# Modulation computed four column tiles at a time, and some loads and steps of row group B rescheduled

## The reference, cut to what matters

```
m = silu(c) @ w_ada + b_ada            # w_ada 2048 x 12288, split into sh1 sc1 gt1 sh2 sc2 gt2
h = rmsnorm(x, g1) * (1 + sc1) + sh1
q, k, v, u, g = split(h @ w_in)        # w_in 2048 x 5120
att = three dilated windows of attention, 8 heads; the samples also read a cache of 2048 positions
mix = concat(att, gelu(u) * spatial_mix(layernorm(gelu(g))))
x = x + gt1 * (mix @ w_out)
h2 = rmsnorm(x, g2) * (1 + sc2) + sh2
idx, gate = top 16 of 16384 experts for each row and each of 8 heads, from h2 @ w_query
x = x + gt2 * sum over the 128 chosen (gate * gelu(h2 . expert_u[idx])) * expert_v[idx]
y = rmsnorm(x, g_final)
```

## Time and profile before

| | us |
|---|---|
| median of 3 runs | 3915.32 (3914.49 to 3929.38) |
| the profiled execution's own time | 3915.24 |
| its span, first to last instruction | 3913.5 |

### The profile page before, as it was taken

One profiled execution on the slowest core, in us unless ns is written; L12 is line 12 of the kernel. 1 busy time (PEld: TensorE's weight loads), 2 busy tenths in 40 slices (PEclk: granted clock), 3 DMA queues, 4 the chain that ended last, 5 costly groups with the idle time before them and its releaser, 6 DMA issues.

```text
span 3913.5 us, 27375 instructions
## 1 busy us (share of the span) xinstructions
PE 2883.8 (74%) x8370; PEld 1221.3 (31%) x8370; DVE 2571.7 (66%) x3880; ACT 613.6 (16%) x1431; POOL 1643.8 (42%) x1178
## 2 busy tenths in 40 slices
PE   6999897979999966677779788855555555555555
PEld 2333443643334333233333255511111111111110
DVE  3200114896677878555555677899988998777676
ACT  1000211210111122233310011211111111000010
POOL 2000001434443455333344364455556665566554
PEclk9999998989999978888889889977877777777778
DMA  9899755899999999999999999999999999999997
GB/s 355 304 328 334 273 193 217 343 408 385 412 412 412 393 390 415 420 419 419 419 407 379 415 397 413 417 420 420 419 418 411 401 413 420 419 420 420 420 416 305
DMA packets 305618, 1506.76 MB, mean 385 GB/s; under 512 B 25343, under 2 KB 25343, under 8 KB 155559
## 3 DMA queue, kind: packets, MB, share of 16 engines
q0 software_dynamic: 160048, 1150.87, 71.8%
q1 hardware_dynamic: 142306, 336.46, 23.1%
q10 hardware_dynamic: 3120, 17.70, 1.1%
HBM read 1490.31 MB, written 13.80 MB: 384 GB/s over the span
## 4 chain that ended last, share of the span: by engine, by line
DMA 46%; PE 40%; issue 6%; DVE 5%; POOL 1%; ACT 1%; SPq 0%; POOLq 0%; DVEq 0%; ACTq 0%
DMA arena<-in_expert_v_dram,arena 39%; PE ps L915 12%; PE ps L734 8%; PE ps L515 7%; PE ps L684 4%; DMA arena<-in_w_in_dram 3%; PE ps L616 3%; POOL arena L2145 1%; DMA arena<-in_w_ada_dram 1%; PE ps L727 1%; PE ps L503 1%; DMA arena<-in_w_out_dram 1%; DMA arena<-in_w_query_dram 1%; PE ps L473 1%; DVE arena L1861 1%
## 5 line engine op out<-in xcount | busy, mean ns | idle before, releaser
L915 PE MATMUL ps<-arena 128*128 128x512 f32 (+1 forms) x2176 | 1373.3, 770 | 829.8 <-DMA arena<-in_expert_v_dram,arena 806.4
L1913 DVE CUSTOM_DVE_ANT_0 arena<-arena 128x2048 f32<-128x2048 f32 x544 | 1246.3, 2291 | 416.9 <-DMA arena<-in_expert_u_dram,arena 411.7
L2145 POOL DMA_INDIRECT arena<-in_expert_v_dram,arena x544 | 901.5, 1657 | 1089.2 <-PE ps L915 843.0
L915 PEld LDWEIGHTS ps<-arena 128*128 128x128 f32 (+1 forms) x2176 | 452.0, 225 | 1667.3 <-issue 1444.4
L2145 POOL DMA_INDIRECT arena<-in_expert_u_dram,arena x544 | 696.2, 1280 | 600.8 <-DVE arena L1913 364.9
L1861 DVE SCALAR_TENSOR_TENSOR arena<-arena 128x1024 f32<-128x1024 f32 x539 | 691.4, 1283 | 240.3 <-issue 216.4
L734 PE MATMUL ps<-arena 128*128 128x512 f32 x896 | 401.9, 602 | 0.0
L1298 ACT ACTIVATE arena<-arena 128x128 f32<-128x128 f32 (+1 forms) x544 | 204.3, 392 | 1096.1 <-PE ps L915 951.8
L515 PE MATMUL ps<-arena 128*128 128x512 f32 x640 | 287.5, 607 | 6.0 <-DMA arena<-in_w_in_dram 6.0
L734 PEld LDWEIGHTS ps<-arena 128*128 128x128 f32 x896 | 166.8, 191 | 238.2 <-issue 237.3
L684 PE MATMUL ps<-arena 128*128 128x288 f32 (+1 forms) x896 | 213.8, 398 | 3.1 <-DMA arena<-in_w_query_dram 1.8
(11 more groups left out here) (228 smaller groups left out, 1525.0 us busy)
## 6 DMA issues: line engine op xcount, KB each, us to landing
arena<-in_w_ada_dram SPq DMA_DIRECT2D x96, 1024.0 KB, 14.2
arena<-in_w_in_dram SPq DMA_DIRECT2D x80, 1024.0 KB, 13.8
arena<-in_w_query_dram SPq DMA_DIRECT2D x36, 1024.0 KB
arena<-in_w_out_dram SPq DMA_DIRECT2D x32, 1024.0 KB, 5.1
arena<-in_cache_k_dram SPq DMA_DIRECT2D x24, 1024.0 KB
arena<-in_cache_v_dram SPq DMA_DIRECT2D x24, 1024.0 KB, 13.2
arena<-in_expert_u_dram,arena POOLq DMA_INDIRECT x544
arena<-in_expert_v_dram,arena POOLq DMA_INDIRECT x544
```

Of the source, the lines that this page charges most:

```text
L915: ins = MM(ps[0:rows, c, :], diag[t % 4][:, 0:rows], v_slot[t % RING][:, c * NC:(c + 1) * NC], start=(j == 0), stop=last, skip_group_check ...
L1913: V.tensor_tensor_reduce(out=u_slot[s % RING], in0=u_slot[s % RING], in1=h2[b], scale=1.0, scalar=0.0, op0=ALU.mult, op1=ALU.add, accum_ou ...
L2145: nc.gpsimd.indirect_dma_start(out=slot[s % RING], out_offset=None, in_=table, in_offset=bass.IndirectOffsetOnAxis(ap=idx, axis=0),).then_ ...
```

## The change

- `w_ada` is read in six **groups** of four tiles. A load is now one block of 128 weight rows by 2048 columns (`ada_source`: pieces of 8 KB; groups 0 and 1 take 1024 columns of the shift part and 1024 of the scale part, pieces of 4 KB). The four column groups of the array take the same block of rows with four different tiles (`ada_block`), and the sum over 16 blocks builds up in the bank. There is no copy to `partial` and no fold: DVE adds the bias for all four tiles at once from the bank (`ada_group`), with bias and gain rows laid out over 128 partitions. Block 0 of group n waits until DVE has done group n-1 (`mod_ready`).
- The turn is four [128, 128] pieces for a group, with four copies, and `quarter_ready` comes in two steps instead of four.
- The list is mixed finely: 16 blocks of group 0, four times (4 blocks, one `w_in` quarter), and then each of the 28 remaining `w_in` quarters behind two or three blocks.
- DVE's index tables are made before the first group and behind the second.
- Group B's first norm moves from step 4 to step 13 (`T_NORM1`), the second head's choice of block 0 from step 1 to step 5 (`TOP_0`), and the loads of B's x rows from behind w load 6 to behind w load 9.
- Blocks 2 and 3 are modulated by ACT as it copies the turned rows from PSUM (32 instructions of 128x128, with bias and scale, instead of 8 copies of 128x512 on ACT and 16 instructions on DVE). PE itself waits for these copies before B's projection.
- `T_IN` is 0.2 steps later, `T_ATT` 3 steps later, heads are 3.75 instead of 4 steps apart.
- Before B's output projection the gate rows and one x block are issued before w loads 1 and 2; two x blocks stay ahead of w load 3, and the sample rows of the second norm move behind w load 4.

```
+add_ada(0, KD)
+for _i in range(4):
+    add_ada(KD + 4 * _i, KD + 4 * _i + 4)
+    add_in(_i % 2, _i // 2)
+_rest = [(_i % 2, 2 + _i // 2) for _i in range(4)] + [(_i, _q) for _i in range(2, 8) for _q in range(4)]
+for _n, (_i, _q) in enumerate(_rest):
+    _upto = 2 * KD + 4 + (4 * KD - 4) * (_n + 1) // len(_rest)
+    add_ada(_ada, _upto)
+    _ada = _upto
+    add_in(_i, _q)
...
-T_NORM1 = 21.0
+T_NORM1 = 13.0
-T_IN = 34.6
+T_IN = 34.8
-T_ATT = t_in(IN_T - 1, 3) + 4.0
+T_ATT = t_in(IN_T - 1, 3) + 7.0
-    return T_ATT + 4.0 * h
+    return T_ATT + 3.75 * h
-TOP_0 = [0, 1.0, 12.2, 14.8, 18.4, 21.0, 24.8, 27.4]
+TOP_0 = [0, 5.0, 12.2, 14.8, 18.4, 21.0, 24.8, 27.4]
...
+            def ada_block(n, k):
+                w = r_quarter(("ada", n), k)
+                if k == 0 and n:
+                    pe.wait_ge(mod_ready, n)
                 for j in range(4):
-                    ins = MM(ps[QUAD * j:QUAD * j + QUAD, 4, :], c_t[:, 4 * q + j, :], w[:, j, :], start=(q == 0), stop=(q == 3))
+                    ins = MM(ps[QUAD * j:QUAD * j + QUAD, 4, :], c_t[:, k, :], w[:, j, :], start=(k == 0), stop=(k == KD - 1))
                 ins.then_inc(wr_used, 1)
...
                     if n < 2:
-                        pe.wait_ge(quarter_ready, q + 1)
+                        pe.wait_ge(quarter_ready, q // 2 + 1)
...
+                        if name == "hb" and b < NB_P:
+                            bank = wait_turn_full(act, (name, b, g))
+                            for k in range(4):
+                                shift, scale = (mod_t[:, part, 4 * g + k, 0:1] for part in range(2))
+                                ins = A.activation(dst[:, 4 * g + k, cols_b(b)], ps[:, bank, k * P:(k + 1) * P], ACT.Identity, bias=shift, scale=scale)
+                            turn_taken(ins, (name, b, g))
...
+            def ada_group(n):
+                m = mod_row[n % 4]
+                wait_group(dv, n)
+                dv.wait_ge(bada_loaded[n % 4], 32 if n < 2 else 16 if n < 4 else 48)
+                link(V.tensor_tensor(m, ps[:, 4, :], m, ALU.add))
+                if n < 2:
+                    dv.wait_ge(in_g1, 32)
+                    link(V.scalar_tensor_tensor(out=m[2 * QUAD:P, :], in0=m[2 * QUAD:P, :], scalar=1.0, in1=g1_rows[n][2 * QUAD:P, :],
+                                                op0=ALU.add, op1=ALU.mult))
+                if n == 4:
+                    dv.wait_ge(in_g2, 16)
+                    link(V.scalar_tensor_tensor(out=m, in0=m, scalar=1.0, in1=g2_rows, op0=ALU.add, op1=ALU.mult))
+                dv.sem_inc(mod_ready, 1)
...
-                yield T_TURN1 + 2.3
-                for b in (2, 3):
-                    for g in range(4):
-                        wait_turn_taken(dv, ("hb", b, g))
-                for k in range(KD):
-                    if k == 8:
-                        yield T_TURN1 + 2.8
-                    link(V.tensor_scalar(h_tb[:, k, 0:2 * P], h_tb[:, k, 0:2 * P], mod_t[:, 1, k, 0:1], mod_t[:, 0, k, 0:1], ALU.mult, ALU.add))
-                yield T_TURN1 + 3.3
+                yield T_TURN1 + 2.6
...
-                if u == 6:
+                if u == 9:
                     sp.wait_ge(norm_h, 4)
                     for i, b in enumerate((2, 3, SB)):
                         sp.dma_start(x_b[i][0:ROWS[b], :], x_of[b]).then_inc(xb_loaded, 16)
...
             wait_turn_full(sp, ("kt", H * DECB - 1, 1))
             load_w(W_OUT, quarter(w_out_v, 0, 0))
+            load_mod(2, gate1_bp, gate1_bs, gate1b_loaded, gate1b_loaded)
+            sp.wait_ge(ss_full, H * DECB)
+            load_x(1)
             sp.wait_ge(os_full, 2 * DECB - 1)
             for u in range(1, 3):
                 load_w(W_OUT + u, quarter(w_out_v, u // 4, u % 4))
-            load_mod(2, gate1_bp, gate1_bs, gate1b_loaded, gate1b_loaded)
             wait_turn_full(sp, ("ot", DECB - 1))
-            for i, b in enumerate((2, 3, SB)):
-                sp.dma_start(x_b[i][0:ROWS[b], :], x_of[b]).then_inc(x1b_loaded, 16)
-            load_mod(4, None, scale2_bs, None, mod2s_loaded)
-            load_mod(3, None, shift2_bs, None, mod2s_loaded)
+            load_x(0)
+            load_x(2)
             for u in range(3, 4 * OUT_T):
+                if u == 5:
+                    load_mod(4, None, scale2_bs, None, mod2s_loaded)
+                    load_mod(3, None, shift2_bs, None, mod2s_loaded)
                 load_w(W_OUT + u, quarter(w_out_v, u // 4, u % 4))
```

More of the change, by code:

```diff
@@ L59, with add_in, add_ada @@
 W_RING = 3
-ADA_SEQ = [4, 0, 5, 1, 6, 2, 7, 3] + list(range(8, ADA_T))
+GROUPS = 6
 QUARTERS = []
[L66 to L76, removed]
+def add_in(i, *quarters):
+    QUARTERS.extend(("in", i, q) for q in quarters)
+def add_ada(first, last):
+    QUARTERS.extend(("ada", u // KD, u % KD) for u in range(first, last))
+add_ada(0, KD)
[3 more added lines that the diff above has]
+_rest = [(_i % 2, 2 + _i // 2) for _i in range(4)] + [(_i, _q) for _i in range(2, 8) for _q in range(4)]
+_ada = 2 * KD
+for _n, (_i, _q) in enumerate(_rest):
[3 more added lines that the diff above has]
+    add_in(_i, _q)
+assert _ada == GROUPS * KD
 EARLY = len(QUARTERS)
-add_tiles(*(("in", i) for i in range(8, IN_T)), *(("out", n) for n in range(OUT_T)))
+for _i in range(8, IN_T):
+    add_in(_i, 0, 1, 2, 3)
+QUARTERS += [("out", n, q) for n in range(OUT_T) for q in range(4)]
 QUARTER_AT = {key: i for i, key in enumerate(QUARTERS)}
-assert sum(kind == "ada" for kind, n, q in QUARTERS) == 4 * ADA_T
+assert len(QUARTER_AT) == len(QUARTERS)
 IN_A = ["g0", "g1", "q0", "q1", "k0", "k1", "v0", "v1", "u0", "u1"]
@@ L1953, in _, with ada_source @@
                 sp.dma_start(h_a[b], x_of[b]).then_inc(xa_loaded[b], 16)
-            for u, (kind, n, q) in enumerate(QUARTERS):
-                table = {"ada": w_ada_v, "in": w_in_v, "out": w_out_v}[kind]
-                tile = {"ada": ADA_SEQ, "in": [COL0[t[0]] + int(t[1]) for t in IN_A], "out": range(OUT_T)}[kind][n]
-                load_r(u, quarter(table, tile, q))
+            def ada_source(n, k):
+                if n < 2:
+                    cols = w_ada_v[:, k, 0:2 * D].rearrange("p (t n) -> p t n", t=2)[:, :, n * 2 * NC:(n + 1) * 2 * NC]
+                    return cols
+                return w_ada_v[:, k, n * D:(n + 1) * D]
+            for u, (kind, n, q) in enumerate(QUARTERS):
+                if kind == "ada":
+                    load_r(u, ada_source(n, q))
+                else:
+                    table = {"in": w_in_v, "out": w_out_v}[kind]
+                    tile = {"in": [COL0[t[0]] + int(t[1]) for t in IN_A], "out": range(OUT_T)}[kind][n]
+                    load_r(u, quarter(table, tile, q))
             sp.wait_ge(o_full, H)
@@ L2070, in _, with spread @@
                                          pattern=[[-1, P]], channel_multiplier=1))
+            def spread(row, *dims):
+                return bass.AP(row.tensor, row.offset, [*dims, [0, QUAD], [1, NC]])
             def load_bada(n):
-                tile = ADA_SEQ[n]
-                pool.dma_start(mod_row[n % 4], b_ada[0, tile * NC:(tile + 1) * NC].partition_broadcast(1 + DECB)).then_inc(bada_loaded[n % 4], 16)
+                if n < 2:
+                    for part in range(2):
+                        rows = slice(2 * QUAD * part, 2 * QUAD * (part + 1))
+                        pool.dma_start(mod_row[n][rows, :], spread(b_ada[0, part * D + n * 2 * NC:], [NC, 2])).then_inc(bada_loaded[n], 16)
+                else:
+                    pool.dma_start(mod_row[n % 4], spread(b_ada[0, n * D:], [NC, 4])).then_inc(bada_loaded[n % 4], 16)
             step(nc.gpsimd.memset(wd_in, 0.0))
```

164 lines of the change are left out of this document (68 added, 96 removed).

## The result

The changed kernel takes 3888.71 us (median of 5 runs, 3888.14 to 3890.32) against 3915.32 us (5 runs, 3914.49 to 3929.38): a ratio of 0.9924, 95% interval 0.9913 to 0.9935. That is 26.6 us faster. The prediction was 3848, range 3824 to 3884: the sign was right, the size 41 us too large, and the time lies 5 us above the range. The profiled execution has a span of 3887.0 us.

A forecast was written before the change was run, and what follows sets the result against it. It took the stream behind slice 8 as bound by its transferred bytes and the early stage as alternating between load and PE limits. From 3915.24, -43 -14 -4 -5 -5 +4 = -67 gave 3848 us, range 3824 to 3884.

The forecast's parts named there:

- Early stage: Up to tile 8's first product: it starts at 392 instead of 435.1 us, -43 (-28 to -47), carried to the stream whole.
- bias and gain rows over 128 partitions are 1.0 MB more ..., 3.7 us: Before the first `w_in` quarter: 1.0 MB more for groups 0 to 3 and 0.4 MB for gains delay it 3.7 us.
- The next step, from there to tile 8: From `w_in` tile 0, quarter 2 at 136 us to tile 8: PE-bound at full clock, 256 us, 54 blocks of 0.90.
- The waits at the two group boundaries: Early stage: block 0 waits for DVE's addition at two boundaries inside a run of blocks, 1.3 us each, 2.6.
- Rival 1: Early stage: pieces of 8 KB load no faster, so it ends at 399 and the kernel takes 3855 us; chance 0.15.
- Start of the stream: Moving B's x rows, first norm and the second choice lets DVE run steps 0 to 7 without a wait: -14 us.
- the query is about 10 us earlier: Start of the stream: query load 7, for which PE waits 10.70 us behind the x rows, comes about 10 us earlier.
- rival 2: The stream gives nothing back, its holes move instead of closing: 3876 us; chance 0.17.
- Modulation of B: 7.37 us of DVE go, ACT gets 32 instructions of 9 to 12.5 us; half the hole closes: -4 us.
- Attention of B: First head: three steps more give ordinary work while K and V land, against PE's 24.75 us wait: -5 us (0 to -6.6).
- Output projection: B's w load 3 lands behind 4 MB of rows, of which 2.75 MB go elsewhere: -5 us (0 to -9.8).
- Late index: Block 2's first index comes at step 254 instead of 252, POOL stands some 7 to 10 us: +4 us (0 to +10).

The follow-up runs named there:

- bias32: The changed kernel with each group's bias and gain rows loaded by four transfers, each one 2 KB row to 32 partitions: 3875.78 us.
- bias9: As bias32, but each transfer writes only the 9 rows that carry data, the others set to zero once: 3872.53 us.
- b1: The changed kernel with bias9's loads and B's x rows loaded behind query load 11 instead of 9: 3858.43 us (3855.25 to 3863.02).
- b1_spaced: b1 with block 0's query quarters due 1.85 instead of 1.6 steps apart and the choices behind them later: 3856.84 us (3853.91 to 3862.92).

## Why the prediction missed

*Early stage, forecast -43, measured -18.4 (tile 8).* One term was missing, 13.7 us of the 24.7, and the priced ones were 11.0 too small. The run to hold against the forecast is bias32, with the bytes that it priced in a good form:
```profile
81.00 9.40 PE L528 MATMUL ps<-arena 128*128 128x512 f32 x16 [3.11 <-DMA arena<-in_w_in_dram]
...
139.56 9.13 PE L528 MATMUL ps<-arena 128*128 128x512 f32 x16 [0.84 <-DMA arena<-in_w_in_dram]
...
402.99 8.73 PE L528 MATMUL ps<-arena 128*128 128x512 f32 x16
```
81.00 for a forecast of 79, 139.56 for 136, 402.99 for 392. (bias9 comes to 77.85 and 135.68, but with 1.5 MB less than was priced.) The changed kernel starts tile 8 at 416.69, 13.7 us behind bias32. The step that failed is "bias and gain rows over 128 partitions are 1.0 MB more ..., 3.7 us": it priced the bytes (measured 3.3) and not the form, which cost another 12.9 at the end. A transfer whose pattern has an outermost count of 2 or 4 had no row in the prediction, and instead of bounding its cost I took it for ordinary. The next step, from there to tile 8, was priced at 256 us and takes 263.4 in bias32 and 263.3 in bias9. The group view of bias9 for that stretch:
```profile
L528 PE MATMUL ps<-arena 128*128 128x512 f32 x448 | 201.4, 603 | 0.7 <-DMA arena<-in_w_in_dram 0.7
L516 PE MATMUL ps<-arena 128*32 128x512 f32 x464 | 55.8, 598 | 2.7 <-DVEq L1460 2.7
```
464 records, eight to a block, are 58 blocks, where the forecast counted 54 (a slip: it should be 96 less the 38 already done), which is 3.6 us. The first quarter takes 8.75 us (135.68 to 144.37, at a granted clock of 0.81) instead of 7.06, 1.7 us. The remaining 2 us are blocks at some 0.93 instead of 0.90 and short waits. The waits at the two group boundaries, 2.7 us, were forecast at 2.6. Rival 1 doesn't hold: load-bound windows full of `ada_block`s move 394 to 409 GB/s (bias9, 60 to 80 and 100 to 120 us), against the 383 of before.

*Start of the stream, forecast -14, measured +6 to +9 alone and +5 in the changed kernel.* This is as large a miss, 19 to 23 us, and it is of mechanism. Two steps failed. The first is "the query is about 10 us earlier": it took PE's 10.70 us for query load 7 as the price of the x rows ahead of it. With the x rows gone from there PE still waits 8.79 us. SP issues load 7 at 641.36 and it is used at 656.98, 15.6 us later; before, with the x rows issued 10 us ahead of it, these were 663.71 and 681.24, 17.5 us. The ring has three slots, so load 7 could be issued only when load 4 had been used, wherever the x rows stood. The second is what was not asked: which load comes behind the x rows in their new place. It is load 10, of the queries of heads 2 and 3, issued at 662.23, and PE stood for it 15.31 us with the v products behind. Where that is repaired, the gain is 6 to 10 us and not 14. PE is nearly full in this stretch; I had that row (59.15 of 60 us from 740 us on) and used it for rival 2 but not in the sum. Rival 2, "its holes move instead of closing", named this half, but at a price of nothing; the hole grew.

*Modulation of B, forecast -4, measured -5.2.* Right, within the runs' spread. ACT's 32 instructions, 11.4 us busy, came within their bounds of 9 to 12.5 us (490 ns is the time of one by itself; they overlap):
```profile
L1115 ACT ACTIVATE arena<-ps,arena 128x128 f32<-128x128 f32 x32 | 11.4, 490 | 1.0 <-PE ps L486 1.0
```
*Attention of B, forecast -5, measured -8.6.* Right in mechanism, too small in size. The measured gain also lies above the bound of 6.6, which was one window's shortage.

*Output projection, forecast -5, measured -3.3*, not told apart from the forecast.

*Late index, forecast +4, not settled.* The wait came about as forecast (7 to 10 us; 11.02 in the changed kernel, 9.46 in b1). The transfers lost 4.4 us around it in the changed kernel and 1.5 in b1, where removing the wait showed no effect. The price of a wait depends on what else is in flight, and that differed between two kernels that are alike there.

The terms as measured for the changed kernel: early stage alone -36.5, given back by the loads' form and bytes +16.2, start +9.3, modulation -5.2, attention -8.6, output projection -3.3, index 0. They make -28.1; the kernel moved by -26.6. They come from different sets and the last four were measured on top of the repairs, so that they meet within 2 us is in part luck; with 4.4 for the index they would make -23.7. Against the forecast of -67, the early stage accounts for 23 us of the 41 and the start for 23, while the others come out 7 better; 1.5 us are left over between the sum and the kernel.

The best version run is b1, 3858.43 us, which is 59 us under the kernel before in its set (ratio 0.9851, 0.9832 to 0.987) and 30 under the changed one (of another set). b1_spaced, 3856.84, isn't told apart from it.

## What to carry to other kernels

A small load written in another shape is a new instruction: ask for its pattern's outermost count and not only for its bytes, because 1.5 MB of rows in such a form held back the weight loads of another queue for 40 us. Before a wait for a load is put down to what stands ahead of it in the queue, look up when it could be issued at all. When a large load is moved behind load n, look up who needs load n+1 and what is queued behind that instruction on its engine. In a kernel bound by its transfers, price a wait by the GB/s missing around it. Then undo the part and compare the ends, measured together, since per-step times shift with the weight loads between them.

## What the runs showed of the hardware

Transfers with an outermost count of 2 or 4 on POOL's queue held up the weight loads of SP's queue as well (31.9 us to landing instead of 22.6), while the DMA share stayed at 1.05: the share does not tell a slow form from full use, only GB/s beside it does (266 against 394 in neighbouring windows with shares of 1.05 and 1.03). Which engines carry such a load can't be seen in these traces. Loads in 4096-byte packets ran faster than loads in 2048-byte ones: 166 ns a packet (bias9) against 88 (before), medians on SP's queue from 10 to 60 us, so 24.7 bytes in a ns against 23.3.
